# One step of a hybrid decoder layer: cached values in quarters, combination and convolution split moved to VectorE, constants loaded once

## The reference

```
h = rms_norm(x)
q, k, v, xb, yb, ga, gb = split(h @ w_in)          # q, k normalised per head
a = DilatedSWA(q, k, v) @ w_oa                      # 12 heads: 3 groups x 4, head size 128
b = (RGLRU(conv4(xb)) * gelu(yb)) @ w_ob
x = x + (sig(ga) * a + sig(gb) * b) @ w_o
x = x + relu(rms_norm(x) @ w_up)**2 @ w_down
x = x + sigmoid(rms_norm(x) @ w_pg) * (p @ w_pe)
```

```
xc = b_conv + sum_j w_conv[j] * xcat[:, j:j+t]
r, i = sigmoid(blockwise xc @ w_rg_a + b), sigmoid(blockwise xc @ w_rg_i + b)
log_a = 8 * r * log_sigmoid(lam);  a = exp(log_a)
h[t] = a[t] * h[t-1] + sqrt(1 - a[t]**2) * (i * xc)[t]
```

## Time and profile before

| | |
|---|---|
| median of 3 runs (lowest, highest) | 2303.85 us (2303.47, 2304.22) |
| the profiled execution | 2304.08 us |
| its span, first to last instruction | 2302.3 us |
| mean granted clock of PE over it | 0.97 |
| PE busy | 2231.4 us (97%) |
| DVE, ACT, POOL busy | 762.8, 650.0, 644.6 us |
| attention, first cached key to last cached value | 108.4 to 817.5 us |
| recurrence, first constants to last scan | 932.4 to 1180.8 us |

### The profile page before, as it was taken

One profiled execution on the slowest core, in us unless ns is written; L12 is line 12 of the kernel. 1 busy time (PEld: TensorE's weight loads), 2 busy tenths in 40 slices (PEclk: granted clock), 3 DMA queues, 4 the chain that ended last, 5 costly groups with the idle time before them and its releaser, 6 DMA issues.

```text
span 2302.3 us, 31867 instructions
## 1 busy us (share of the span) xinstructions
PE 2231.4 (97%) x13686; PEld 2182.4 (95%) x13686; DVE 762.8 (33%) x1211; ACT 650.0 (28%) x1080; POOL 644.6 (28%) x281
## 2 busy tenths in 40 slices
PE   7999989999999999999999999999999999999998
PEld 5999989989989999999899999999999999999998
DVE  6332263255246124366661332121121121121223
ACT  5332333333233222355551222210111111012231
POOL 0110141131022143344432224342242243233431
PEclk9998999999989999999999999999999999999999
DMA  8122223223223221211111122111111111111132
GB/s 264 50 88 86 93 73 123 63 85 132 66 70 123 87 89 43 59 43 34 43 47 46 47 75 84 40 44 55 37 46 55 37 46 46 47 47 46 46 131 75
DMA packets 58335, 162.00 MB, mean 70 GB/s; under 512 B 10043, under 2 KB 22183, under 8 KB 56627
## 3 DMA queue, kind: packets, MB, share of 16 engines
q1 hardware_dynamic: 58196, 159.97, 21.8%
HBM read 142.22 MB, written 20.09 MB: 70 GB/s over the span
## 4 chain that ended last, share of the span: by engine, by line
PE 48%; DVE 1%; ACT 1%; POOL 0%; issue 0%; DMA 0%; ACTq 0%; DVEq 0%; SPq 0%
PE ps L1387 48%; POOL w_lo L1636 0%; PE pair L1395 0%; DVE z L1749 0%; ACT b_hi L1521 0%; POOL act_lo L1670 0%; DVE lru_h L1746 0%; DMA lru_prm<-lru_prm 0%; DVE x_res L1700 0%; DVE tmp L1695 0%; DVE tmp L1698 0%; ACT L1561 0%; ACT L1507 0%; ACT L1534 0%; DVE tmp L1803 0%
## 5 line engine op out<-in xcount | busy, mean ns | idle before, releaser
L1636 POOL TENSOR_TENSOR w_lo<-w_raw,w_hi 128x1024 fp32r<-128x1024 f32 (+1 forms) x119 | 293.0, 2462 | 452.2 <-ACT w_hi L1454 452.2
L1050 PE MATMUL ps<-act_lo,w_hi 128*128 128x352 f32 x1056 | 367.3, 348 | 9.8 <-issue 5.5
L1050 PE MATMUL ps<-act_hi,w_hi 128*128 128x352 f32 x1056 | 351.0, 332 | 0.0
L1050 PE MATMUL ps<-act_hi,w_lo 128*128 128x352 f32 x1056 | 350.8, 332 | 0.0
L1387 PE MATMUL ps<-act_lo,w_hi 128*128 128x352 f32 x1536 | 335.1, 326 | 15.4 <-ACT xcat_s L1467 12.2
L1387 PE MATMUL ps<-act_hi,w_lo 128*128 128x352 f32 x1536 | 333.0, 324 | 0.0
L1387 PE MATMUL ps<-act_hi,w_hi 128*128 128x352 f32 x1536 | 332.4, 325 | 0.0
L711 POOL TENSOR_TENSOR w_lo<-w_raw,w_hi 128x1024 fp32r<-128x1024 f32 (+1 forms) x44 | 105.7, 2401 | 624.6 <-ACT w_hi L749 624.6
L1387 PEld LDWEIGHTS ps<-act_lo,w_hi 128*128 128x128 f32 x1536 | 263.6, 190 | 17.6 <-issue 13.8
L1387 PEld LDWEIGHTS ps<-act_hi,w_lo 128*128 128x128 f32 x1536 | 265.5, 189 | 0.0
L1387 PEld LDWEIGHTS ps<-act_hi,w_hi 128*128 128x128 f32 x1536 | 262.4, 189 | 0.0
(11 more groups left out here) (228 smaller groups left out, 2375.5 us busy)
## 6 DMA issues: line engine op xcount, KB each, us to landing
w_raw<-w_qkv SPq DMA_DIRECT2D x36, 512.0 KB, 4.3
w_raw<-w_up SPq DMA_DIRECT2D x32, 512.0 KB, 3.6
w_raw<-w_down SPq DMA_DIRECT2D x32, 512.0 KB, 3.6
vcache<-vc SPq DMA_DIRECT2D x12, 1024.0 KB, 5.1
kcache<-kc SPq DMA_DIRECT2D x16, 512.0 KB, 3.9
e_bc<-lse_dram SPq DMA_DIRECT2D x12, 528.0 KB, 5.6
x_res<-x_t SPq DMA_DIRECT2D x8, 528.0 KB, 10.2
pe_dram<-pe_stage SPq DMA_DIRECT2D x8, 528.0 KB, 3.7
```

Of the source, the lines that this page charges most:

```text
L1050: ins = pe.matmul(pj[c][:, 0:CH], w[:, b % 2, k], x[:, k, c * CH:(c + 1) * CH], start=k == 0 and x is act_lo, stop=k == KD - 1 and w is w_lo)
L1636: pool.tensor_tensor(w_lo[:, s, 0:nk], w_raw[:, s, 0:nk], w_hi[:, s, 0:nk].bitcast(F32), ALU.subtract).then_inc(S["wlo"], 1)
```

## The change

1. *Prologue.* The bias rows go to five banks instead of two, and only the last waits for a copy. DVE copies two of them, then makes `p_lo` and `wp_lo`, then copies the other four. ACT evicts all embedding tiles, from alternating banks.
2. *Samples' cached values.* They leave pair 4 of `values` and become `sample_values(s, part)`: the new rows and the first quarter in slot 8 of step s, the other three quarters in slots 0 to 2 of the next step. The output of pair 4 is copied in slot 3 of that step. The cache of values has two buffers in the residual's place (`X`, not needed until the gates are written there), and one transfer per step, issued in slot 3 of the step; the transfers of cached keys no longer wait for the values of the step before.
3. *Combination of heads.* Subtraction and weighing go from POOL to DVE, spread over the slots: maxima in 3 and 4, subtraction in 5 to 7, the exponential in 8, sums of weights in 0 and 1 of g = 1, weighing and adding in 2 to 4. The reciprocal becomes exp(-ln) on ACT in slot 2. The combined head is stored in slot 6 instead of 4.
4. *Recurrence.* The constants of all tiles are loaded once, in two halves (`prm_a`, `prm_b`), after ao 7. `xc_lo` and `ri * xc` go from POOL to DVE.

The core of the diff:

```diff
+    def bias_bank(g, c):
+        n = 2 * g + c
+        return pair[0:HG, n % 5, 0:HTB] if n % 5 < 2 else ps[1][0:HG, n % 5 - 2, 0:HTB]
...
+        n = 3
+        for m in range(4, KD):
+            for x in range(n, n + 3):
+                split_h(*divmod(x, KD))
+            n += 3
+            evict_pin(m)
+        for x in range(n, NCH * KD):
+            split_h(*divmod(x, KD))
...
+        copy_bias(0)
+        copy_bias(1)
         for k in range(PKD):
+            split("p", p_lo, p_raw, p_hi, k)
...
+            split("wp", wp_lo, wp_raw, wp_hi, k)
+        for n in range(2, 2 * NG):
+            copy_bias(n)
...
-    vc = nc.alloc_sbuf_tensor_at("vcache", [P, 16, HD], F32, offset=kc_at)
+    vc = [nc.alloc_sbuf_tensor_at(f"vcache{n}", [P, NS, HD], F32, offset=shared["x_at"] + n * (4 * KD * T - 4 * NS * HD)) for n in range(2)]
-    vc2 = nc.alloc_sbuf_tensor_at("vcache2", [P, 16, HD], F32, offset=e_at)
...
-                wait(sp, "o_psum", PAIRS * s)
                 sp.dma_start(kc[:, i % 2, 0:n, 0:CK[g]], a[f"kc{g}"][j, :, n * i:n * (i + 1)]).then_inc(S[f"kc{i % 2}_loaded"], 16)
-            if i == 3 and CSLOT[g] > 16:
-                wait(sp, "prod", 3 * j)
-                wait(sp, "den", j)
-                sp.dma_start(vc2[0:CK[g]], a[f"vc{g}"][j, :, 16:32]).then_inc(S["vc_loaded"], 16)
-            if i == 6:
-                sp.wait_ge(S["kc_used"], 4 * (s + 1))
-                n = min(16, CSLOT[g])
-                sp.dma_start(vc[0:CK[g], 0:n], a[f"vc{g}"][j, :, 0:n]).then_inc(S["vc_loaded"], 16)
+            if i == 3:
+                if s < 2:
+                    sp.wait_ge(S["h_hi"], NCH * KD)
+                    sp.wait_ge(S["h_lo"], NCH * KD)
+                wait(sp, "o_psum", PAIRS * (s - 1))
...
+        def invert(jj):
+
+            act.wait_ge(S["den"], jj + 1)
+            act.activation(mx[:], mx[:], ACT.Ln).then_inc(S["den_ln"], 1)
+            act.wait_ge(S["den_ln"], jj + 1)
+            act.activation(mx[:], mx[:], ACT.Exp, scale=-1.0).then_inc(S["rec"], 1)
...
+        def less_max(jj, g):
+            dve.wait_ge(S["mxd"], jj + 1)
+            if g == 0:
+                dve.tensor_tensor(e[:, 0], e[:, 0], mx[:], ALU.subtract).then_inc(S["sub"], 1)
+            else:
+                eg = shaped(e[:, g], g, "group")
+                dve.tensor_tensor(eg, eg, in_group_order(mx, g), ALU.subtract).then_inc(S["sub"], 1)
+                dve.tensor_tensor(e[:, g, NP_:T], e[:, g, NP_:T], mx[:, NP_:T], ALU.subtract).then_inc(S["sub"], 1)
...
+        def weigh(jj, g):
+            dve.wait_ge(S["ex"], jj + 1)
+            dst = o_of(jj, g)
+            dve.tensor_tensor(dst[:], dst[:], e[:, g], ALU.mult).then_inc(S["prod"], 1)
...
+                if g == 0 and j:
+                    if i in (3, 4):
+                        max_lse(j - 1, i - 2)
+                    elif i in (5, 6, 7):
+                        less_max(j - 1, i - 5)
+                if g == 1 and j:
+                    if i < 2:
+                        denominators(j - 1, i + 1)
+                    elif i == 2:
+                        weigh(j - 1, 0)
+                        weigh(j - 1, 1)
+                    elif i == 3:
+                        weigh(j - 1, 2)
+                        combine(j - 1, 0)
+                    elif i == 4:
+                        combine(j - 1, 1)
 
...
+        def sample_values(s, part):
+
+            g = s % NG
+            n = PAIRS * s + PAIRS - 1
+            if part == 0:
+                pe.wait_ge(S["pt_ready"], n + 1)
+                pe.wait_ge(S["o_ready"], n)
+                pe.wait_ge(S["vc_loaded"], 16 * (s + 1))
+                pe.matmul(pO[:, 0:NS], v[0:NS, TL], pt[0:NS, 1, 0:NS], start=True, stop=False,
+                          skip_group_check=True).then_inc(S["new_used"], 1)
+            w = NS // CSLOT[g]
+            quarter = CSLOT[g] // 4
+            for c in range(part * quarter, (part + 1) * quarter):
+                ins = pe.matmul(pO[:, c * w:(c + 1) * w], vc[s % 2][0:CK[g], c], pt[0:CK[g], 0, c * w:(c + 1) * w],
+                                start=False, stop=True, skip_group_check=True)
+            if part == 3:
+                ins.then_inc(S["o_psum"], 1)
...
+                if core and i == SLOTS - 1:
+                    sample_values(cur, 0)
+                if 1 <= cur <= NSTEP and i < 3:
+                    sample_values(cur - 1, i + 1)
...
-            sp.wait_ge(S["mm"], done("ao", KD - 1))
-            wait(sp, "z", m - 1)
-            wait(sp, "save", m - 1)
-            sp.dma_start(prm[:, m % 2], a["lru_prm"][m]).then_inc(S[f"prm{m % 2}_loaded"], 16)
+            if m == 0:
+                sp.wait_ge(S["mm"], done("ao", KD - 1))
+                sp.dma_start(prm_a[:], a["lru_prm"][:, 0:KD // 2]).then_inc(S["prm_loaded"], 16)
+                sp.dma_start(prm_b[:], a["lru_prm"][:, KD // 2:KD]).then_inc(S["prm_loaded"], 16)
...
-                pool.wait_ge(S["xc_hi"], m + 1)
-                pool.tensor_tensor(xc_lo[:], xc[:], xc_hi[:].bitcast(F32), ALU.subtract).then_inc(S["xc_lo"], 1)
-            elif name == "ri":
-                wait_evicted(pool, name, m)
-                pool.tensor_tensor(ri[:], ri[:], xc[:], ALU.mult).then_inc(S["ix"], 1)
...
+            wait_evicted(dve, "ri", m)
+            dve.tensor_tensor(ri[:], ri[:], xc[:], ALU.mult).then_inc(S["ix"], 1)
...
+        def split_conv(m):
+            dve.wait_ge(S["xc_hi"], m + 1)
+            dve.tensor_tensor(xc_lo[:], xc[:], xc_hi[:].bitcast(F32), ALU.subtract).then_inc(S["xc_lo"], 1)
...
                     decay(m - 1)
                     conv(m)
                     recur(m - 1)
+                split_conv(m)
```

More of the change, by code:

```diff
@@ L125, in build @@
         act_lo = alloc("act_lo", [P, KD, T], F32R)
+        x_at = cursor[0]
         X = alloc("x_res", [P, KD, T])
@@ L317, in scalar @@
             act.activation(wp_hi[:, k], wp_raw[:, k], ACT.Copy).then_inc(S["wp_hi"], 1)
-        for k in range(4):
+        for k in range(5):
             square(k)
         evict_pin(0)
-        for k in range(4, KD):
+        for k in range(5, KD):
             square(k)
-        evict_pin(2)
+        evict_pin(1)
         act.wait_ge(S["w0_loaded"], 16)
@@ L450, in tensor @@
             for c in range(2):
-                if g:
-                    pe.wait_ge(S["bias_copied"], 2 * g - 1 + c)
-                pe.matmul(pair[0:HG, c, 0:HTB], relb[:, HG * g:HG * (g + 1)], sel[:, g, c * HTB:(c + 1) * HTB],
+                if (g, c) == (NG - 1, 1):
+                    pe.wait_ge(S["bias_copied"], 1)
+                pe.matmul(bias_bank(g, c), relb[:, HG * g:HG * (g + 1)], sel[:, g, c * HTB:(c + 1) * HTB],
                           start=True, stop=True).then_inc(S["bias_psum"], 1)
-        for m in range(4):
+        for m in range(3):
             embed(m)
@@ L458, in tensor @@
         pe.wait_ge(S["sum_x"], KD)
-        pe.wait_ge(S["bias_copied"], 2 * NG)
         column_sum(0)
         column_sum(1)
-        embed(4)
+        embed(3)
         column_sum(2)
-        for m in range(5, KD):
+        for m in range(4, KD):
             embed(m)
-        for s in range(2):
-            pe.wait_ge(S[f"pev{s}"], KD // 2)
+        pe.wait_ge(S["pev"], KD)
         pe.wait_ge(S["ln_x"], NCH)
@@ L1299, in hidden, with prm @@
         return G[2 * (m % 2)]
+    def prm(m, at, end):
+        half = prm_a if m < KD // 2 else prm_b
+        return half[:, m % (KD // 2), at:end]
     def sync(sp):
@@ L1495, in gate_a @@
             act.wait_ge(S["mm"], done("ra", m))
-            act.activation(c2(ra[:, 0:NP_]), pair[:], ACT.Sigmoid, bias=prm[:, m % 2, 1:2]).then_inc(S["ev_a"], 1)
+            act.activation(c2(ra[:, 0:NP_]), pair[:], ACT.Sigmoid, bias=prm(m, 1, 2)).then_inc(S["ev_a"], 1)
         def gate_i(m):
```

177 lines of the change are left out of this document (62 added, 115 removed).

## The result

The changed kernel takes 2205.59 us (median of four, 2204.05 to 2209.71), the kernel before 2304.03: a ratio of 0.9576, 95% interval 0.9559 to 0.9593. The forecast was 2237 with a range of 2212 to 2266: the direction was right and the gain, 98 us, half as large again as forecast.

A forecast was written before the change was run, and what follows sets the result against it. TensorE was busy 2231.4 of 2302.3 us, so only its waits and lower clock could be won. Samples' values -19, heads -20, last head -4, recurrence -17, prologue -7 sum to -67: from 2304.1 to 2237 us, range 2212 to 2266.

The forecast's parts named there:

- The samples' values: Sample-value matmuls in quarters behind four projections: less time at the lower clock, -19 us (from -31 to -7).
- I take eight, 12.2: Of group 1's sixteen quarters, eight are still followed by a slow stretch, costing 12.2 us (bounds 0 and 24.3).
- +3.2: Samples' values: 0.09 us for each of 36 new starts of runs, 3.2 us lost.
- step 0's 1.95 us: Time of sixteen sample-value records at full clock, used to price all twelve stretches at 103.2 us, leaving 34.6 to the clock.
- the heads: Combination of heads in the attention: waits for DVE and the slow clock behind them go, -20 us (from -27 to -13).
- The new wait: Slot 2 of group 1: TensorE waits for ACT's square behind its logarithm and exponential, 2.3 us per head, +7 in all.
- The recurrence: Constants loaded once: ACT's and TensorE's waits and the slow matmuls behind them go, -17 us (from -18 to -10).
- The prologue: Embedding's wait for its weight split goes, and a third of the wait for DVE's last eviction, -7 us (-4 to -10.9).
- the last head: TensorE's wait for a weight split queued behind POOL's products goes, with the clock behind it, -4 us (-4.4 to 0).
- Rival 4: All is better: no slow quarter and ACT in time, 2218 us, or 2215 with a whole prologue; chance 0.06.
- rival 3: The clock does not care for the length of sample-value runs, so their term is about +0: 2256 us; chance 0.05.
- Rival 5: Slower than before: each of 48 quarters breaks the clock; 2298 us at 1.52 each, 2371 at 3.04; chance 0.04.

The follow-up runs named there:

- the kernel with one run: Changed kernel with all four quarters of the samples' cached values in slot 8 again, one behind the other; measured 2246.5 us, 40.9 more than the changed kernel.

## Why the prediction was wrong

**The samples' values, the step that failed.** It said "I take eight, 12.2", "+3.2" for new starts, and priced the higher clock from step 0's 1.95 us. Undoing the cut costs 40.9 us; the forecast had 19, with a bound of 31. All three numbers were too dear. One slow stretch stands behind a quarter in the profiled execution, not eight, and up to five in other kernels. New starts cost nothing that can be seen: a quarter with its projection takes 5.79, of which 4.05 is the projection by the prediction's count, so 1.74 for sixteen records. Their starts in the timeline say nearly that, 202.44 - 200.73 = 1.71:

```profile
200.73 1.84 PE L1139 MATMUL pair<-pt,vcache 128*128 128x1 f32 x16
202.44 0.41 PE L1049 MATMUL ps<-act_lo,w_hi 128*128 128x352 f32 x1
```

And with 1.74 in place of 1.95 the twelve stretches of the earlier trace rows would take 97.3 us at the higher clock instead of 103.2, so the clock's share was 40.5, not 34.6: a duration in a timeline holds the start and the end that overlap the neighbours, and multiplying it counts them each time. The granted clock would have told it: each stretch's length times what its clock lacks to 1.00, as the prediction did for the heads (9.58 x (1 - 0.77)), comes to 41.1 over the twelve. The mechanism was right; its size was wrong on every side in the same direction, and bounds made of the same 1.95 could not hold it. (The 0.61 that the prediction gives for thirty-two columns is the first of four such runs; the other three stood at 0.68.)

**Beside the steps.** The place of b in SBUF gave 7 us. The diff showed it, since the buffer ahead of b changes its size; the prediction read the new layout for its transfers only. With it and the samples' values right, the sum would be -67 - 22 - 7 = -96. The range could not hold that either: all five terms at their best bounds come to -91, 2213 us, and the dense phase has no term in it. (Put together as independent, the bounds give about 15 us to either side, not 25.)

**The heads.** In the attention 62.4 - 40.9 = 21.5 us are left for them, forecast 20. The normalisation behind the subtraction of slot 7 now takes 0.29 us; the same tile took 2.55 beside POOL before (first line), and two larger ones took 5.39 in the earlier trace rows:

```profile
319.56 2.55 DVE L903 TENSOR_SCALAR L<-L,rsum 32x160 f32<-32x160 f32 x1
295.75 2.03 DVE L952 TENSOR_TENSOR e_bc<-e_bc,mx 128x1024 f32<-128x1024 f32 x1
297.97 0.29 DVE L884 TENSOR_SCALAR L<-L,rsum 32x160 f32<-32x160 f32 x1
```

The explanation was too narrow: it took POOL for the cause, and undoing either half of the edit brings no wait back, so the near number is partly luck. The new wait was foreseen in its place and was smaller, 1.20 us per head where 2.3 were counted; what ACT does, and the wait of TensorE behind it:

```profile
324.08 1.07 ACT L780 ACTIVATE mx<-mx 128x1056 f32<-128x1056 f32 x1
325.18 1.09 ACT L782 ACTIVATE mx<-mx 128x1056 f32<-128x1056 f32 x1
327.15 0.45 ACT L724 ACTIVATE qk_sq<-ps 128x352 f32<-128x352 f32 x1
```

```profile
327.64 0.86 PE L1057 MATMUL ps<-qk_sq,ones 128*128 128x352 f32 x2 [1.20 <-ACT qk_sq L724]
```

In this execution no slow stretch follows; in four of the other kernels one follows all three.

**The recurrence.** -19.2, forecast -17, for a reason that was half right: "because their load waits for the recurrence before it" is true, but the recurrence was late by POOL. The prediction named the scan without POOL's passes as an exchange and did not follow it to the load. That the number came close is luck in part.

```profile
L1760 DVE TENSOR_TENSOR_SCAN lru_h<-lru_a,lru_b x8: 2357/2358/2358, 910.2 to 1089.4; 128x1056 f32<-128x1056 f32 x8
```

**The prologue and the last head.** -6.4 for -7, -3.5 for -4. Nothing was undone here; the table and the waits alone speak for these two. The embedding starts at 14.78, where 14.8 was worked out from the earlier trace rows:

```profile
14.78 1.22 PE L441 MATMUL ps<-p_lo,wp_hi 128*128 128x352 f32 x3 [0.23 <-DVE wp_lo L382]
```

Rival 4 (all is better, 2218 or 2215) had 0.06 and was the nearest; rival 3 (the clock does not care for the length of runs) is refuted by the kernel with one run. Rival 5's price of 1.52 for each of 48 quarters came for one.

## What to carry to other kernels

Look for stretches where an engine is busy and its clock is low: 97% busy hid some 60 us. Many one-column matmuls in a row cost twice, in themselves and in the dense work behind them; cut such a run until no slow stretch follows, mind other narrow runs close by, and judge by several executions. When a wait goes, undo each half of the edit: twice here either half would have done, and only one was free.

## What the runs showed of the hardware beyond that

- The pace of 72 fp32 matmuls of 352 columns in an unbroken chain in the dense phase is 11.52, 11.65 or 11.68 us, and goes with where the moving operand lies relative to the stationary one, modulo 128 bytes; one change of 64 bytes is worth 7 us of 2300. Why is open; only offsets of 32, 0 and -32 were seen.
- Which run of sixteen records is followed by a slow stretch changes with edits elsewhere in the program (group 1's quarters, 1 to 5 of 16 in a profile), but only the first and the fourth quarter of a step ever are (23 of 80; the two between, none of 80). What sets it was not settled.
- A two-input pass of POOL stretches DVE's normalisation even when nothing waits for it: 439 ns on average instead of 312.
